# Long convolution by a split transform: the filter's spectrum formed once and arranged by ScalarE, and the forms moved one pair ahead

## The reference, cut to what matters

```python
h = sin(...) @ w_o                         # filter samples, forward and backward half
decay = exp(-t * deltas[None, :])          # t: position, deltas: one rate per channel
h_fwd, h_bwd = h[:, :D_A] * decay, h[:, D_A:] * decay
l1 = sum(|h_fwd|) + sum(|h_bwd[1:]|)
k = concatenate([h_fwd, 0, reversed(h_bwd[1:])]) / (l1 + EPS)

U = rfft(v * x1, n=2 * L)
K = rfft(k)
y = irfft(U * K, n=2 * L)[:, :L] + (v * x1) * skip
y_a = x0 * y * silu(gate)
```

## Time and profile before

| | |
|---|---|
| median of 3 runs | 3340.97 us (3327.26 to 3345.0) |
| profiled execution | 3344.58 us, its span 3342.8 us |
| mean granted TensorE clock | 0.968 |
| PE busy | 3086.8 us, 92% |
| DVE busy | 2504.9 us, 75% |
| ACT busy | 804.9 us, 24% |
| POOL busy | 299.0 us, 9% |
| DMA | 392.21 MB, mean 117 GB/s |
| long convolution | 2387 us to about 2975 us of the span |

### The profile page before, as it was taken

How to read it: one execution, slowest core, us unless ns; L and a number is a source line. 1 busy time by engine, 2 the same in 40 slices (tenths; PEclk the granted TensorE clock), 3 DMA queues, 4 the chain that set the end, 5 groups by cost and what they waited for, 6 DMA issues and landing times. The chain is left out here.

```text
span 3342.8 us, 33360 instructions
## 1 busy us (share of the span) xinstructions
PE 3086.8 (92%) x13138; PEld 2238.6 (67%) x13138; DVE 2504.9 (75%) x2672; ACT 804.9 (24%) x1394; POOL 299.0 (9%) x420
## 2 busy tenths in 40 slices
PE   6999999889885989999999999999898999979999
PEld 4444444656774767787888888787566666777887
DVE  6979999597995796999999999975456667552221
ACT  2000000585333321000011111112353735431110
POOL 3211220000112350000000000000000000000000
PEclk9999999999997999999999999999999999979999
DMA  6565551201437454665545454521211120334321
GB/s 202 145 178 149 141 149 44 108 1 54 133 129 225 136 151 120 162 179 156 162 139 145 136 141 134 143 76 34 112 54 51 54 101 13 138 116 142 100 88 53
DMA packets 206060, 392.21 MB, mean 117 GB/s; under 512 B 20224, under 2 KB 132032, under 8 KB 198032
## 3 DMA queue, kind: packets, MB, share of 16 engines
q1 hardware_dynamic: 186000, 319.27, 31.2%
q0 software_dynamic: 18752, 62.42, 7.3%
q10 hardware_dynamic: 1152, 8.39, 0.7%
HBM read 312.41 MB, written 81.81 MB: 118 GB/s over the span
## 5 line engine op out<-in xcount | busy, mean ns | idle before, releaser
L1665 PE MATMUL PS<-HH,WH 128*128 128x512 f32 x1536 | 605.4, 394 | 40.2 <-DVE WL L1562 23.0
L1667 PE MATMUL PS<-HH,WL 128*128 128x512 f32 x1536 | 604.9, 394 | 0.0
L1666 PE MATMUL PS<-HL,WH 128*128 128x512 f32 x1536 | 604.2, 393 | 0.0
L782 PE MATMUL PS<-M 128*128 128x512 f32 x1152 | 502.3, 598 | 16.2 <-DVE M L605 13.6
L782 PEld LDWEIGHTS PS<-M 128*128 128x128 f32 x1152 | 220.4, 192 | 297.4 <-issue 279.8
L1665 PEld LDWEIGHTS PS<-HH,WH 128*128 128x128 f32 x1536 | 290.2, 189 | 110.3 <-DVE WL L1562 19.0
L1666 PEld LDWEIGHTS PS<-HL,WH 128*128 128x128 f32 x1536 | 290.2, 189 | 64.1
L1667 PEld LDWEIGHTS PS<-HH,WL 128*128 128x128 f32 x1536 | 290.3, 189 | 62.9
L109 DVE SCALAR_TENSOR_TENSOR HP<-MF,HP 128x1024 f32<-128x1024 f32 x252 | 323.4, 1283 | 8.0
L2394 PE MATMUL PS<-WH,YH 128*128 128x512 f32 x512 | 200.9, 392 | 14.7 <-DVE WL L2365 9.5
L109 DVE SCALAR_TENSOR_TENSOR M<-M 128x1024 f32<-128x1024 f32 x160 | 205.6, 1285 | 7.2 <-DMA M<-c_feat 1.5
(11 more groups left out here) (220 smaller groups left out, 5110.7 us busy)
## 6 DMA issues: line engine op xcount, KB each, us to landing
MF<-h_scratch SPq DMA_DIRECT2D x380, 256.0 KB, 4.3
M<-c_feat POOLq DMA_DIRECT2D x194, 256.0 KB, 4.3
MF<-w_in SPq DMA_DIRECT2D x56, 512.0 KB, 4.7
M<-u_scratch SPq DMA_DIRECT2D x16, 1024.0 KB, 4.8
M<-w_in SPq DMA_DIRECT2D x18, 512.0 KB, 4.8
M<-x SPq DMA_DIRECT2D x16, 512.0 KB, 4.4
x_scratch<-M SPq DMA_DIRECT2D x16, 512.0 KB, 5.3
h_scratch<-M SPq DMA_DIRECT2D x16, 512.0 KB, 5.8
```

Of the source, the lines that this page charges most:

```text
L782: ins = t.matmul(PS[:, banks + c, :], wt[:, k], HT[:, k, TC * c:TC * c + TC], start=(k == 0), stop=(k == KD - 1))
L1665: t.matmul(dst, wh, hh, start=(k == 0), stop=False)
L1666: t.matmul(dst, wh, hl, start=False, stop=False)
L1667: ins = t.matmul(dst, wl, hh, start=False, stop=(k == KD - 1))
```

## The change

- STRIP holds [re, im] per bin, 128 columns instead of 256. A pair takes four matmuls instead of six: the filter's spectrum into one bank, the input's into another, each [re; im] on the partitions and both bins side by side. `kf_done` and `uf_done` take the place of `uk_done` and `b_done`.
- Pairs go round three sets of two banks (`banks_of`); the forms of pair n + 1 are issued ahead of `inverse(n - 1)`.
- ACT makes the arrangement that the product needs from the one filter bank with four copies of 64 partitions x 512: the real rows to both halves of KS[.., 0], the imaginary rows to both halves of KS[.., 1], the second time with the sign changed. KS has three slots instead of two.
- DVE makes the products in three instructions: U times KS[.., 0] on 128 partitions, and the two halves of U, exchanged, times KS[.., 1] on 64 partitions each. The subtraction is as before.
- The decay factors of chunks 1 to 3 come from a new constant tensor `c_decay`, loaded by POOL's queue into DEC, which has four slots instead of two. ACT makes only those of chunk 0.
- Tiles in M are moved to make room; `c_fft` has 8192 columns instead of 12288; a wait for `yc_done` moves from pair 1 to pair 2.

```diff
+        def banks_of(n):
+            return 2 * (n % 16 % 3), 2 * (n % 16 % 3) + 1
...
+        @block.gpsimd
+        def _(g):
+            for kq in range(16, 16 * NCH):
+                g.wait_ge(k_weighted, kq - 3)
+                g.dma_start(DEC[kq % 4], A["c_decay"][kq - 16]).then_inc(decay_in[kq % 4], 16)
...
         ACT, in the loop over pairs
-                    bank = 3 * (n % 2)
-                    s.wait_ge(uk_done, n + 1)
-                    if n >= 2:
-                        s.wait_ge(pm_done, n - 1)
+                    bank, ks = banks_of(n)[0], KS[:, p % 3]
+                    s.wait_ge(kf_done, n + 1)
+                    if n >= 3:
+                        s.wait_ge(pm_done, n - 2)
                     for to in range(2):
-                        s.activation(KS[HID * to:HID * to + HID, n % 2, :, CH:2 * CH],
-                                     PS[HID - HID * to:P - HID * to, bank:bank + 2, 0:CH], ACT.Copy).then_inc(ks_done, 1)
+                        s.activation(ks[HID * to:HID * to + HID, 0], PS[0:HID, bank, :], ACT.Copy).then_inc(ks_done, 1)
+                    for to in range(2):
+                        s.activation(ks[HID * to:HID * to + HID, 1], PS[HID:P, bank, :], ACT.Copy,
+                                     scale=1.0 - 2.0 * to).then_inc(ks_done, 1)
...
-                    s.wait_ge(b_done, n + 1)
-                    s.activation(KS[:, n % 2, :, 0:CH], PS[:, bank + 2, :].rearrange("p (y c) -> p y c", y=2),
-                                 ACT.Copy).then_inc(ks_done, 1)
-                    if cc + 1 < NCH:
-                        decays(n + 16)
...
         DVE, in weighted(kq)
-                v.wait_ge(decay_done, 2 * kq + 2)
+                if cc:
+                    v.wait_ge(decay_in[kq % 4], 16 * ((kq - 16) // 4 + 1))
+                else:
+                    v.wait_ge(decay_done, 2 * kq + 2)
...
         DVE, in the loop over pairs
+                    u, ks = PS[:, banks_of(n)[1], :], KS[:, p % 3]
+                    v.wait_ge(uf_done, n + 1)
                     v.wait_ge(ks_done, ks_count(n))
                     if n:
                         v.wait_ge(y_done, n)
-                    v.tensor_tensor(PM, PS[:, bank:bank + 2, :], KS[:, n % 2], ALU.mult).then_inc(pm_done, 1)
+                    v.tensor_tensor(PM[:, 0], u, ks[:, 0], ALU.mult)
+                    v.tensor_tensor(PM[0:HID, 1], u[HID:P], ks[0:HID, 1], ALU.mult)
+                    v.tensor_tensor(PM[HID:P, 1], u[0:HID], ks[HID:P, 1], ALU.mult).then_inc(pm_done, 1)
                     v.wait_ge(pm_done, n + 1)
...
         PE, second_stage(cc)
+                def forms(p):
+                    n = 16 * cc + p
+                    if p >= 3:
+                        t.wait_ge(pm_done, n - 2)
+                    if p == 2 and cc:
+                        t.wait_ge(yc_done, 8 * cc)
+                    for src, bank, formed in ((KTB[cc % 2], banks_of(n)[0], kf_done), (UTB, banks_of(n)[1], uf_done)):
+                        for x in range(2):
+                            ins = t.matmul(PS[:, bank, CH * x:CH * x + CH], STRIP[:, 2 * p + x], src[:, p, x], start=True, stop=True)
+                        ins.then_inc(formed, 1)
+
+                forms(0)
                 for p in range(16):
                     n = 16 * cc + p
-                    ...the six matmuls of pair n
+                    if p + 1 < 16:
+                        forms(p + 1)
                     if p:
                         inverse(n - 1)
```

More of the change, by code:

```diff
@@ L1697, in region @@
             return region_of(M, base, *dims)
-        STRIP = region(0, 32, 4 * HID)
-        INV = region(8192, 32, P)
+        STRIP = region(0, 32, P)
+        INV = region(4096, 32, P)
+        KS = region(8192, 3, 2, 512)
         KB = [region_of(KX, 0, 32 * CH), region(12288, 32 * CH)]
         UIN = region(20480, S)
-        DEC = [region(22528 + 512 * i, 512) for i in range(2)]
-        KABS = [region(23552 + 512 * i, 512) for i in range(2)]
+        DEC = [region(22528 + 512 * i, 512) for i in range(4)]
+        KABS = [region(11264 + 512 * i, 512) for i in range(2)]
         KSUM = region(24576, 512)
         WOC = [region_of(CC, 0, CH), region(25088, CH)]
-        DELTA = [region_of(CC, CH, CH), region(25088 + CH, CH)]
+        DELTA = region_of(CC, CH, CH)
         TNEG = region_of(CC, 2 * CH, 32)
@@ L1757, in long_convolution @@
         decay_done = sem("decay_done")
+        decay_in = [sem("decay_in%d" % i) for i in range(4)]
         k_weighted = sem("k_weighted")
@@ L1866, in decays @@
             def decays(kq):
[L1867 to L1874, removed]
+                if kq == 0:
+                    s.wait_ge(kept.first_in, 64)
+                if kq >= 4:
+                    s.wait_ge(k_weighted, kq - 3)
                 for x in range(2):
-                    s.activation(DEC[kq % 2][:, CH * x:CH * x + CH], DELTA[cc % 2], ACT.Exp,
-                                 scale=TNEG[:, 2 * j + x:2 * j + x + 1]).then_inc(decay_done, 1)
+                    s.activation(DEC[kq % 4][:, CH * x:CH * x + CH], DELTA, ACT.Exp,
+                                 scale=TNEG[:, 2 * kq + x:2 * kq + x + 1]).then_inc(decay_done, 1)
             def absolute(kq):
@@ L2542, in constants @@
     c["c_delta"] = np.abs(np.linspace(lo, hi, D).astype(np.float32))
+    later = c["c_delta"].reshape(NCH, 1, 1, 1, CH)[1:]
+    c["c_decay"] = np.exp(later * c["c_tneg"].T.reshape(1, 16, 2, P, 1)).transpose(0, 1, 3, 2, 4).reshape(-1, P, 2 * CH).copy()
     return c
```

25 lines of the change are left out of this document (11 added, 14 removed).

## The result

The changed kernel took 3308.36 us (median of 8 runs, 3292.09 to 3317.05) where the one before took 3335.47 us (8 runs, 3326.84 to 3345.0). The ratio is 0.9915, with a 95% interval of 0.9891 to 0.9939. The prediction was 3306 us, with 3295 to 3326 as its range. It was right, in time and in sign. The spans of the profiled executions differ by 3342.8 - 3309.3 = 33.5 us, the medians by 27.1, where the sum of the prediction was 35.

What follows compares the result with a forecast made beforehand. PE at full clock was taken to bound the second-stage pairs. Savings of 12.0, 11.3, 11.3 and 0.4 us in chunks 0 to 3 sum to 35: 3341 - 35 = 3306 us, range 3295 to 3326.

Steps and rivals of the forecast that it cites:

- PE's part: Second-stage pairs: form passes fall from 12 to 8, 0.91 us less; 3.98 us with generation, 2.72 without.
- ACT's part: Second-stage pairs: four half-partition copies, no exponentials in the loop; 3.46 to 3.7 us, under PE's 3.98.
- DVE's part: Second-stage pairs: three products at 0.71 us plus subtraction, weighting and summing, 3.97 us; 3.65 with products at 0.60.
- The rival in which DVE takes the bound: Chunks 0 to 2: slower products make the period 4.3 us, 14 us less saved, about 3320 us; chance 0.17.
- The path through the engines: Loop over PE, ACT, DVE and back: needs 3.75 us a pair with generation, 3.55 without, ruling chunk 3.
- The rival in which this loop rules everywhere: All chunks: slower hand-overs make the period 4.35 us, chunk 3 4.1; 24 us given back, about 3330; chance 0.08.
- The sum: Savings by chunk in the second stage: 12.0, 11.3, 11.3 and 0.4 us for chunks 0 to 3, 35 us together.
- their growing: Stretches between second-stage chunks, from last inverse to next first: growth there would show the prediction wrong; no size given.
- The clock in chunk 3: Rival: PE, busy only 77% in chunk 3, drops to half clock; 29 us given back, 3335 us; chance 0.06.
- The late tiles: Rival, chunks 0 to 2: decay loads land late, at 24 us the period is 6.2; 62 us lost, 3400; chance 0.04.
- Profile and median: Whole kernel: profiled 3344.6 us would become 3309.6; the median of runs, 3341.0, lies 3.6 below, giving 3306.

Runs made afterwards that it cites:

- the third experiment: Kernel before, with only the decay factors of chunks 1 to 3 loaded by POOL's queue into its two slots; ratio 0.9994 to the kernel before.
- the first: Changed kernel with the forms of pair n issued in their own iteration, not one pair ahead; ratio 0.9998 to the kernel before.
- fourth experiment: Changed kernel with, in chunk 3, two banks for the inverse and ACT copying it out one pair later; 3300.09 us, ratio 0.9888.
- second experiment: Changed kernel with ACT making the decay factors of all chunks in the loop and POOL loading nothing; ratio 0.9981 to the kernel before.

## Why the prediction was right

**PE's part** held to the hundredth: eight passes and 3.98 us a pair with generation, and 256 passes fewer. The experiments without the summing, with half the generation and with both show that PE's part sets the period. I took 4.00, for three limits that stand close; the real period is PE's own and nothing is added where they meet. That made the forecast of chunks 1 and 2 0.1 us short each.

**ACT's part.** The sum of 3.46 to 3.7 us was right: ACT was busy for 40.75 of 47.73 us, 3.4 a pair, and put the period nowhere, while the same loop with the exponentials in it ran into 4.42.

**DVE's part.** The bounds were 0.60 and 0.71 for a product, and 0.71 was taken from what ACT's copies did; the steps behind the first and the second product are 0.70 to 0.71, and 0.60 to 0.61 with whole tiles. (Three products at 0.60 make DVE's sum 3.63, not 3.65.) The choice mattered little, since PE's 3.98 stands above either sum; it shows in chunk 3, as 7.11 us against 6.91. Here this case's rows bear out the rule of the Trainium skill, "VectorE: DVE Perf Modes", section "Two Vector instructions with no wait between them": an instruction in another quadrant than the last is held. The section doesn't say what a hold costs; here it is 0.1 us. DVE's whole pair is 3.93, 0.04 under the 3.97 taken, since the weighting and the summing step by 0.59 to 0.61. The rival in which DVE takes the bound missed by 0.05 us a pair: DVE has no slack, but it isn't the limit.

**The path through the engines** was 3.75 with generation, and 3.82 is measured with both engines lightened; without generation it was 3.55, and 3.555 is measured. The rival in which this loop rules everywhere falls with it. In chunk 3 it rules, as the forecast itself said, and the second bank for the inverse shows what is in it: 8.3 us.

**The sum.** 12.0, 11.3, 11.3 and 0.4 stand against 11.95, 11.42, 11.38 and 0.38. Of the 1.6 us that the executions lack against it, 1.05 had come about before the second stage and 0.5 is in the gaps. I had put the gaps at no change, being the same instructions in the same order, and had named their growing as a sign that I was wrong. In this one pair of executions they grew by 0.5 us; in others by far more, so this term was off by little through luck. Here are the three gaps of every kernel in which PE is as full in the pairs as in the changed one and the same work fills the gaps, and of the two with the pairs of before (us, mean granted clock in brackets):

| kernel | gap 1 | gap 2 | gap 3 | sum |
|---|---|---|---|---|
| before | 66.58 (1.00) | 68.11 (0.97) | 68.19 (0.97) | 202.9 |
| loads alone, on the kernel before | 66.59 (1.00) | 68.02 (0.97) | 68.21 (0.97) | 202.8 |
| after | 68.90 (0.98) | 69.66 (0.95) | 67.44 (1.00) | 206.0 |
| second bank for the inverse | 69.04 (0.98) | 69.68 (0.95) | 71.62 (0.93) | 210.3 |
| products over 128 partitions | 68.91 (0.98) | 67.26 (1.00) | 67.28 (1.00) | 203.5 |
| two slots | 72.13 (0.93) | 72.20 (0.93) | 72.20 (0.93) | 216.5 |

The length follows the mean clock. How full PE was in the pairs doesn't set it: in the last four kernels PE waits for 1.2 to 1.4 us in twelve pairs, and the sums lie 13 us apart. In the first two it waits for nothing there; whether their gaps are alike for that reason, two profiles can't tell. Nor do the waits of 1.2 to 1.4 and 1.74 us for DVE before the last two inverses of a chunk decide it, since they stand ahead of gaps at 1.00 and at 0.93 alike. What makes PE's clock fall in one gap and not in the other stays open.

**The clock in chunk 3** stayed at 1.00 from 2850.89 to 2886.48 with PE busy 84% (29.82 of 35.59 us). Only the last two inverses, after waits of 2.94 and 0.93 us, ran at half (2.08 and 2.07 us where 1.17 is usual); the last one of before did so too. In other executions the chunk began at half clock as well (without the summing it took 55.25 us at a mean of 0.90, 2.5 us more than after), far from the 29 us of that rival, which is refuted for the chunk as a whole.

**The late tiles** are refuted: 48 loads with a median landing of 2.9 us and a maximum of 6.7, against 16 us of cover, and no weighting waited for a DMA. The rule on descriptors that wait for Vector instructions, which I had set beside this rival ("SBUF — State Buffer" of the Trainium skill, section "A bandwidth-pool intuition that's wrong (but worth ruling out)"), shows nothing here: DVE was busy 95% of the time and the loads landed sooner than in the earlier trace rows. The section's own case is a copy on DVE, though, and in the pairs DVE has only instructions with two input tensors; no run here has a copy beside the loads.

**Profile and median.** The execution before lay 3.6 us above the median of its runs then; over 8 runs the median is 3335.47 and it lies 9 us above. The execution after, at 3311.16, lies 2.8 above its median of 3308.36. So the medians differ by 27.1 us and the spans by 33.5. The second number is what two executions differ by that took the same course and had gaps of nearly the same length. With other gaps it is smaller: the kernel with two slots has the pairs of the changed kernel (3.98 and 3.56 us), and beside the third experiment, of the same course, it saves 3328.2 - 3303.1 = 25.1 us, since its gaps took 13.7 us more than there (2.6 of it the later first inverses) and its chunks 1 and 2 lost 1.6 us each in stretches at half clock. So at full clock the pairs save 35 us, and between 25 and 33.5 us reached the end of these executions. The medians' 27.1 lies within that, and just under the 28 to 42 us of saving that I had forecast. That the forecast of 3306 us came within 2.4 us of the median is in part luck: the median of before was 3335.47 over 8 runs and not the 3341 of three, 5.5 us lower, and the saving was 7.9 us smaller.

## What to carry to other kernels

When one engine is full, work out the other engines and the loop through them with the new sum before moving work: here the pairs got the saving of 0.91 us in full since DVE (3.93) and the loop (3.82) ended just under PE's 3.98, and with the move ahead or the decay loads left out the ratio of the medians stayed within 0.2% of the kernel before. Where no engine is full, as in chunk 3, lighter engines give little (0.08 of 0.91 us); break the loop instead, with a second bank and a copy one step later. And before a difference between two executions is put down to an edit, compare the stretches that the edit doesn't touch, with their granted clock: here they alone differed by up to 13 us. A loop's length has to be divided by the number of items in it, and that number is read from the order of the instructions.

## What the runs showed of the hardware

Half-partition DVE instructions last as long as whole ones (0.68 us for 512 elements) and, where they alternate halves, step by 0.70 to 0.71 instead of 0.60 to 0.61.

Loads of 256 KB issued by POOL landed in 2.7 to 6.7 us (median 2.9) beside a DVE that was 95% busy. One slot was enough but for the first pairs of chunks 1 and 2, which I had not expected.

The runs of the kernel before fall in two groups whose means lie 15 us apart: 3326.55 to 3333.36 and 3337.27 to 3348.7 in 29 runs. Those of the kernel after may do the same (3292.09 to 3298.47 and 3304.56 to 3317.05 in 8). The profiles show a place for it, far from the change. These are the waits of PE for DVE's line 605 in the stretch from 200 to 600 us, of the kernel before and then of the kernel after (us, times, longest):

```profile
PE PS L782 <- DVE M L605: 13.6, 3, 6.6
```

```profile
PE PS L782 <- DVE M L605: 12.6, 3, 6.0
```

The profiles of the first, third and fourth experiment above, spans 3326.2, 3328.2 and 3292.2, have a busier PE there (396.52, 394.74 and 396.31 of 400 us, where both kernels compared have 385.42 and 386.47). All twelve profiles fall on one side or the other: in five PE is busy for 385.4 to 386.7 us there and the first form of chunk 0 comes at 2454.7 to 2457.7, in seven for 394.6 to 396.5 and the first form comes at 2436.1 to 2442.0. So an execution takes one course or the other before the second stage begins. The time alone doesn't tell which: the kernel with two slots took the shorter course and, with its long gaps, 3304.97 us. Both profiled executions of the comparison are of the longer course, so that their 33.5 us are free of it, while it widens the intervals of the ratios; the fourth and the third experiment, both of the shorter course, differ by 36.0. What tips an execution to one course wasn't tested.

The granted clock varies between executions of the same instructions, and the length of a stretch with it: the third gap took 67.44 us at 1.00 and 71.62 at 0.93 behind the same three chunks. In the last four rows of the table above the three gaps together took 203.5 to 216.5 us. The kernels in which PE waited for 3.2 us and more in twelve pairs, and whose gaps hold the same work (first and second experiment, and the one with half the generation), had 210.2, 211.5 and 210.6, in the midst of that. So no run shows that a lighter PE in the pairs costs clock behind them.
